# Input projection of twelve of sixteen token tiles in pieces inside the mixers; four tiles, key/value columns and compression in one first phase

## The reference

```python
h = rms_norm(x, norm_mix)
z = einsum('bsd,de->bse', h, w_in)                   # 2048 x 3096
(r_q, r_k, r_v, r_g, c_b, c_c, c_h, n_q, n_kc, n_vc, n_ks, n_vs, n_kw, n_vw, n_g) = split(z, ...)
y_ret = retention(r_q, r_k, r_v, r_g)                # 4 heads, chunks of 128, a state from chunk to chunk
y_conv = short_conv(c_b, c_c, c_h, conv_w)           # width 3
y_nsa = nsa(n_q, n_kc, n_vc, n_ks, n_vs, n_kw, n_vw, n_g, ...)
x = x + concat(y_ret, y_conv, y_nsa) @ w_out
x = x + relu(rms_norm(x, norm_mlp) @ w_up)**2 @ w_down
```

## Time and profile before

| | |
|---|---|
| time of runs | 3452.62 us (3452.37 to 3452.97) |
| profiled execution | 3461.74 us, its span 3459.8 us |
| projection | 0 to 583 us of the span |
| compression | 583 to 673 |
| mixers up to the first turned sum of a unit (L1436) | 673 to 797.1 |
| mixers, the next twenty units | 797.1 to 1401.8 |
| mixers, the rest | 1401.8 to 1777.6 |
| output product | 1777.6 to 2028 |
| MLP | 2028 to 3459.8 |
| mean granted TensorE clock | 0.949 of full |

### The profile page before, as it was taken

How to read it: one execution, slowest core, us unless ns; L and a number is a source line. 1 busy time by engine, 2 the same in 40 slices (tenths; PEclk the granted TensorE clock), 3 DMA queues, 4 the chain that set the end, 5 groups by cost and what they waited for, 6 DMA issues and landing times. The chain is left out here.

```text
span 3459.8 us, 43048 instructions
## 1 busy us (share of the span) xinstructions
PE 3198.2 (92%) x15500; PEld 2541.8 (73%) x15500; DVE 1480.1 (43%) x2760; ACT 984.4 (28%) x1621; POOL 1075.4 (31%) x614
## 2 busy tenths in 40 slices
PE   7999998668888899999979969999999999999999
PEld 7999998655555555565548758888788878888887
DVE  3113111046666666766532233336433543354333
ACT  3012000023434444444430032232222322232221
POOL 3222221043423323222010044444444434444442
PEclk9999999657989999999999979999999999999999
DMA  5223222210101001000023342223322232233221
GB/s 173 96 97 102 93 96 84 66 53 33 64 33 63 34 33 64 33 33 7 7 101 137 115 153 97 96 94 119 116 97 97 84 135 97 97 97 122 97 97 61
DMA packets 164983, 291.73 MB, mean 84 GB/s; under 512 B 19167, under 2 KB 126559, under 8 KB 162780
## 3 DMA queue, kind: packets, MB, share of 16 engines
q1 hardware_dynamic: 160252, 273.31, 23.2%
q10 hardware_dynamic: 4608, 16.78, 1.4%
HBM read 239.53 MB, written 50.53 MB: 84 GB/s over the span
## 5 line engine op out<-in xcount | busy, mean ns | idle before, releaser
L1756 POOL TENSOR_TENSOR mlp_down_lo<-mlp_down_raw,mlp_down_hi 128x2048 fp32r<-128x2048 f32 x64 | 298.3, 4661 | 750.5 <-ACT mlp_down_hi L1795 750.5
L1876 DVE TENSOR_TENSOR mlp_y<-mlp_acc,mlp_y 128x512 f32<-128x512 f32 x512 | 344.5, 688 | 201.3 <-PE mlp_acc L1954 196.4
L1954 PE MATMUL mlp_acc<-mlp_down_hi,mlp_f_hi 128*128 128x512 f32 x1024 | 402.4, 393 | 10.7 <-DVE mlp_y L1876 10.7
L1932 PE MATMUL mlp_up<-mlp_hT_hi,mlp_up_hi 128*128 128x512 f32 x1024 | 399.5, 390 | 2.5 <-DVE mlp_hT_lo L1898 2.5
L1954 PE MATMUL mlp_acc<-mlp_down_hi,mlp_f_lo 128*128 128x512 f32 x1024 | 400.0, 391 | 0.0
L1954 PE MATMUL mlp_acc<-mlp_down_lo,mlp_f_hi 128*128 128x512 f32 x1024 | 400.0, 391 | 0.0
L1932 PE MATMUL mlp_up<-mlp_hT_hi,mlp_up_lo 128*128 128x512 f32 x1024 | 399.3, 390 | 0.0
L1932 PE MATMUL mlp_up<-mlp_hT_lo,mlp_up_hi 128*128 128x512 f32 x1024 | 399.2, 390 | 0.0
L1863 DVE TENSOR_TENSOR mlp_f<-mlp_relu 128x512 f32<-128x512 f32 x128 | 133.2, 1042 | 603.2 <-ACT mlp_relu L1802 603.2
L311 PE MATMUL proj_acc<-proj_w_hi,proj_hT_hi 128*128 128x344 f32 x1152 | 369.8, 321 | 10.5 <-issue 9.5
L311 PE MATMUL proj_acc<-proj_w_hi,proj_hT_lo 128*128 128x344 f32 x1152 | 367.8, 319 | 0.0
(11 more groups left out here) (257 smaller groups left out, 5560.0 us busy)
## 6 DMA issues: line engine op xcount, KB each, us to landing
mlp_up_raw<-in_w_up SPq DMA_DIRECT2D x64, 1024.0 KB, 5.2
mlp_down_raw<-in_w_down SPq DMA_DIRECT2D x64, 1024.0 KB, 4.8
proj_w_raw<-in_w_in SPq DMA_DIRECT2D x18, 1376.0 KB, 6.4
z_scratch<-proj_z_out SPq DMA_DIRECT2D x144, 172.0 KB, 1.9
mix_z<-z_scratch SPq DMA_DIRECT2D x16, 1548.0 KB, 6.9
proj_x_tile<-in_x ACTq DMA_DIRECT2D x16, 512.0 KB, 3.9
mixed_scratch<-mix_mixed SPq DMA_DIRECT2D x16, 512.0 KB, 2.9
out_mixed<-mixed_scratch SPq DMA_DIRECT2D x16, 512.0 KB, 4.1
```

The lines of the kernel that those rows point to most:

```text
L1756: nc.gpsimd.tensor_tensor(dn_lo[:, b, :, :], dn_raw[:, :, :], dn_hi[:, b, :, :].bitcast(F32), ALU.subtract).then_inc(dn_lo_done, 1)
L1876: nc.vector.tensor_tensor(y[:, yb, tt, cols], acc[i % AR][:, :], y[:, yb, tt, cols], ALU.add).then_inc(added, 1)
L1932: mm = nc.tensor.matmul(up_ps[t % 2][:, :], w[:, b, k, cols], h[:, k, :], start=k == 0 and w is up_hi and h is h_hi, stop=k == KT - 1 and ...
L1954: mm = nc.tensor.matmul(acc[i % AR][:, :], a[:, b, k, tt * P:(tt + 1) * P], w[:, b, k, c * BANK:(c + 1) * BANK], start=k == 0 and a is f_h ...
```

## The change

**First phase.** `projection_phase` and `compress_phase` become one, `heads_phase`, again with a written list of steps, `HeadsPlan`. It normalises and transposes all sixteen tiles. Tiles 0 to 3 keep their transposed, split rows in SBUF and are multiplied with ten chunks of 284 columns: the 2840 columns of w_in other than n_kc, n_vc. For tiles 4 to 15 the transposed, split rows are stored to DRAM (`turned_scratch`, 1 MB a tile). Every chunk of w_in is loaded and split once, and both parts are stored (`split_scratch`, 2.3 MB a chunk). The 256 key/value columns are made for all tiles with the weights stationary, so that they come out transposed (`pair` steps: one group of four tiles, six of two); they are not stored. The compression steps stand among the last products; the bias rows ride as two more columns of `kvT`. The w1 of keys and of values share one buffer.

**Mixers.** The other 120 products (12 tiles x 10 chunks) are `fill` steps of the plan, each cut in four parts of 6 matmuls, with a `drain` (ACT) and a store (SP) behind it. They go two tiles at a time: two tiles of turned rows are held in SBUF (`held`), and each quarter of a chunk (`w_unit`, 0.58 MB, a ring of five) serves both tiles. 16 fills stand ahead of unit 0, and five in each unit after that until all are placed, which is in unit 20. They use `prep_ps`. z of a tile is loaded in parts (keys two deep, retention and convolution once), keys from tile 4 on only when all stores of its pair of tiles have landed. The prep pieces are sorted: key pieces of tile i + 2 in the unit with g = 0, retention pieces in the one with g = 1. Stores of `mixed` are cut in two. The constants are set and loaded at the start of this phase.

```diff
+T1 = 4
+CHUNKS = 10
+BW = 284
+class HeadsPlan:
+    def __init__(self, tiles):
+        groups = [range(0, 4)] + [range(t, t + 2) for t in range(T1, tiles, 2)]
+        products = [("product", c, t) for c in range(CHUNKS) for t in range(T1)]
+        later = iter(products)
+        for t in range(tiles):
+            steps.append(("tile", t))
+            for g, group in enumerate(groups):
+                if t == group[-1] + 1 or t == tiles - 1 == group[-1]:
+                    steps += [("pair", g, j) for j in range(2)]
+            if t >= T1 - 1:
+                steps.append(next(later))
+        rest = list(later)
+        spread = {1: ("bias rows",), 3: ("first", 0), 6: ("first", 1), 8: ("silu",), 9: ("second",),
+                  11: ("norm",), 13: ("turn",)}
...
 class Plan:
     def __init__(self, tiles):
-        self.steps = self.prep(0) + merge(first, self.prep(1))
+        self.steps = [("load keys", 0), ("load keys", 1), ("load retention", 0)] + self.more(2)
+        self.steps += self.spread(self.prep(0, KEY_PIECES), 2) + [("load keys", 2)]
+        early = self.prep(0, RET_PIECES) + [("store rows", 0), ("load retention", 1)] + self.prep(1, KEY_PIECES) + self.prep(1, RET_PIECES)
+        self.steps += merge(first, self.spread(early, FIRST_FILLS - 4))
...
-            ahead = []
-            if u + 2 < units:
-                pieces = self.prep(i + 2) if i + 2 < tiles else []
-                half = len(pieces) // GROUPS
-                ahead = merge(self.front(u + 2), pieces[g * half:(g + 1) * half])
+            pieces = self.prep(i + 2, (KEY_PIECES, RET_PIECES)[g]) if i + 2 < tiles else []
+            pieces = self.spread(pieces, UNIT_FILLS)
+            ahead = merge(self.front(u + 2), pieces) if u + 2 < units else pieces
+            if g == 0:
+                if i + 1 < tiles:
+                    self.steps.append(("store rows", i + 1))
+                if i + 2 < tiles:
+                    self.steps.append(("load retention", i + 2))
+                if i + 3 < tiles:
+                    self.steps.append(("load keys", i + 3))
...
+    def more(self, n):
+        while n > 0 and self.filled < self.fills:
+            steps += [("fill", self.filled, part) for part in range(PARTS)] + [("drain", self.filled)]
...
+    def spread(self, pieces, n):
+        gaps = [k for k, s in enumerate(pieces) if s[0] != "prep" or not s[2].startswith("read")] + [len(pieces)]
...
 PE of the mixers
+                if kind == "fill":
+                    n, part = step[1:]
+                    if part == 0:
+                        bank_free(("fill", n))
+                        pe.wait_ge(held_in[b], 16 * (pair + 1))
+                    pe.wait_ge(unit_in[unit % WS], 16 * (unit // WS + 1))
+                    for q in range(UNIT_K):
+                        nc.tensor.matmul(prep_ps[:, 0:BW], hi[:, k, :], w_hi[:, q, :], start=k == 0, stop=False)
+                        nc.tensor.matmul(prep_ps[:, 0:BW], lo[:, k, :], w_hi[:, q, :], start=False, stop=False)
+                        mm = nc.tensor.matmul(prep_ps[:, 0:BW], hi[:, k, :], w_lo[:, q, :], ...)
 ACT of the mixers
+                elif kind == "drain":
+                    act.wait_ge(fill_sum, n + 1)
+                    if n >= ZR:
+                        act.wait_ge(z_stored[n % ZR], 16 * (n // ZR))
+                    nc.scalar.copy(z_out[:, n % ZR, :], prep_ps[:, 0:BW]).then_inc(drained, 1)
```

More of the change, by code:

```diff
@@ L348, in chain, with clear_sems @@
+    def clear_sems(self, eng):
+        numbers = sorted(s.num for s in self.taken)
+        assert numbers == list(range(numbers[0], numbers[-1] + 1))
+        eng.sem_clear(range(numbers[0], numbers[-1] + 1))
 def chain(eng, done):
@@ new lines, in _ @@
+            nc.gpsimd.memset(values[:, :, :], 0.0).then_inc(values_cleared, 1)
+            pool.wait_ge(values_cleared, 1)
+            root(0)
+            pool.wait_ge(kv_hi_done, 1)
+            nc.gpsimd.tensor_tensor(kv_lo[:, :, :], w_raw[:, 1, :, 0:KV_WIDTH], kv_hi[:, :, :].bitcast(F32),
+                                    ALU.subtract).then_inc(kv_lo_done, 1)
+            root(1)
+            weights_low(0)
+            for step in plan.steps:
+                if step[0] == "tile":
+                    root(step[1] + 2)
+                elif step[0] == "product" and step[2] == 1:
+                    weights_low(step[1] + 1)
+                elif step[1:] == ("norm",):
+                    pool.wait_ge(cmp_squares, 1)
+                    link(nc.gpsimd.tensor_scalar(mean[:, :], ssq[:, :], 1.0 / HEAD, EPS, ALU.mult, ALU.add))
+                    nc.gpsimd.tensor_tensor(cmp_rstd[:, :], mean[:, :], neg_half[:, :], ALU.pow).then_inc(powered, 1)
@@ L642 @@
+    return m
 CMP, SLC, WIN = 0, 1, 2
@@ L705, in __init__ @@
                 self.steps.append(("post", u - 1, SLC))
+                if g == 0:
+                    self.steps.append(("store heads", i - 1))
             self.steps += own[1:5] + merge(own[5:] + [("values", u, SLC, i), ("lift", u, SLC)], ahead)
-        self.steps += [("turn", units - 1, SLC), ("post", units - 1, SLC)]
+        self.steps += [("turn", units - 1, SLC), ("post", units - 1, SLC), ("store heads", tiles - 1)]
+        assert self.filled == self.fills
+        self.bank_before = {}
+        before = None
+        for s in self.steps:
+            use = s if s[0] == "prep" and s[2].startswith("fill") else s[:2] if s[0] == "fill" else None
+            if use is not None and use != before:
+                self.bank_before[use] = before
+                before = use
         self.scores_n = {}
@@ L777, in mixers_phase @@
     NBLK = S // SLC_LEN
-    assert NBLK == NBLKS
+    KT = turned.shape[3]
+    assert NBLK == NBLKS and KT == PARTS * UNIT_K
     plan = Plan(NT)
@@ L1277, in _, with bank_free @@
         def _(pe):
-            pe.wait_ge(cleared, 1)
+            def bank_free(use):
+                before = plan.bank_before[use]
+                if before is not None:
+                    if before[0] == "fill":
+                        pe.wait_ge(drained, before[1] + 1)
+                    else:
+                        prep_read(pe, before[1], before[2][5:])
+            ready = False
             for step in plan.steps:
```

1288 lines of the change are left out of this document (727 added, 561 removed).

## The result

The changed kernel takes 3497.9 us (median of 4 runs, 3486.3 to 3504.2) beside 3452.8 for the kernel before (3452.4 to 3455.3). The ratio is 1.0125, 95% interval 1.0098 to 1.0153: slower by 45 us. The forecast was 3290, range 3205 to 3395. The profiled execution took 3499.9 us, its span is 3497.9. From here on, "unit" and "first finished unit" are cut at the same instructions as in the earlier trace rows: the first of the four transposes that turn a unit's selected branch.

What follows compares the result with a forecast made beforehand. TensorE was taken to wait for short VectorE and ScalarE chains early in the mixers and to be the bound late. 263 + 138 + 838 + 376 = 1615 for 1777.6, 163 less, gave 3290 us, range 3205 to 3395.

Steps and rivals of the forecast that it cites:

- Start of the first phase, tile part, products: 263: First phase, before the mixers: 23 start, 105 tiles 4 to 15, 125 products and compression, 10 last stores; was 673 us.
- Rival C: First phase bound by its transfers, 64.8 MB at 184 GB/s: 352 us, 89 more, total 3379; chance 0.10.
- To the first finished unit: 138: Mixers' start: 124.1 us becomes 138, as 23 + 37 + 57 + 21, with 21 fills added; ends 120 and 190.
- Units 1 to 20: 838: Mixers' units 1 to 20: 604.7 us becomes 838, as 481 work, 311 fills and 46 idle; ends 790 and 916.
- residual idle 2.3 a unit, 46: Units 1 to 20: TensorE idle left with fills in place, 2.3 us a unit, 46 us for 20 units.
- half of that comes back, 48: Units 1 to 20: 0.16 of the time at half clock; half of that is returned, 48 us.
- The work of 481: Units 1 to 20: work already there, 604.7 less 75.1 idle less 48 for the clock, 481 us.
- The lower count of 455: Units 1 to 20: work counted instruction by instruction at 227 and 112 ns, 455 us; used for the 790 end.
- rival D: Slower: fills' weight ring does not run ahead, 60 pairs each wait for a 5.2 us landing, 312 us; 3602; chance 0.05.
- 375.8 stays: Mixers from unit 21 to the end: unchanged at 375.8 us, since no fill is left and the bytes are the same.
- Rival A: Better cover: units at 790, start 125, first phase 250; 237 us less, 3216; chance 0.15.
- Rival B: Nothing is hidden: units 916, start 190, first phase 263; 33 us less, 3420; chance 0.08.

Runs made afterwards that it cites:

- The best version: Fastest run with all the work: the changed kernel with three edits of order, two of seven prep turns back in the first unit; 3364.4 us, ratio 0.9727.
- Turns shared: Against the kernel with three edits of order: two of the seven prep turns (qq and kz) moved back to the first unit's end; 3364.4 us, ratio 0.9727.
- three edits of order: Changed kernel with key/query turns in the second unit, projection chunk after next loaded earlier, and mixers' start loads reordered; 3370.9 us, ratio 0.9747.

## Why the prediction was wrong, step by step

- **Start of the first phase, tile part, products: 263, was 287.5.** I had named the load of a chunk behind the low part of the one before as a chain of 15.3 us beside 12.6 of matmuls, and charged 2.5 us a chunk for the last four. The queue's order cost 24 more at the fifth chunk, where the load stood behind loads that wait for memsets. With that line mended the phase ends at 263.2. The POOL and ScalarE times were right (4.96 and 2.1 us beside 5.1 and 2.1). Rival C, bound by transfers, is out: the DMA share is 0.68 over the phase and a line's move gave the time back.
- **To the first finished unit: 138, was 207.** Work (103 us at full speed) was right; 504 matmuls of fills at 131 ns and 280 others at 227 or 112 ns give 101. Idle was 76.5 where I had 35 (the 23 less three fills, and 21). Prep of tile 0 began 45 us behind the phase's start (332.6), where I had 23, and I had not seen that the drains wait for the tables too, so that fills can't run meanwhile. And I took full clock: it was 0.79, which by what is left of the 207 cost about 30. The best version still needs 179 to 186; the idle time left there is 54 to 56, and the clock 0.81 to 0.83. What of it could be had by other orders I did not try.
- **Units 1 to 20: 838, was 927.5. This is where the prediction failed**, in its term "residual idle 2.3 a unit, 46" and in "half of that comes back, 48". Idle was 99, and 46 us were lost to the half level, much as before the change (50). I argued that pieces of fills close the short waits and that a unit with 30 us of dense work keeps the clock. But the diff also sorts the prep pieces anew, and the sum has no term for that, not even one of nothing with its cover named. With the turns out of that unit the stretch is 855.7 at 51.8 idle and a clock of 0.98: the forecast's idle term and its returned clock, in a kernel with the order that I had silently assumed.
- **Prices.** The work of 481 held: TensorE was busy 828.5 us, and less 46 for the clock and 311 of fills that is 471. The lower count of 455 at the range's low end is wrong. At 227 ns for each matmul of 512 columns (890 of them) and 112 for the others it gives only about 390, and it leaves out that the 358 value matmuls cost more: here two of them and a score matmul (0.23) take 1.15 us, so one costs about 0.46.

```profile
1168.33 1.07 PE L1683 MATMUL mix_selected<-mix_probs,mix_v_s 128*66 128x512 f32 x2
1168.84 0.80 PE L1653 MATMUL mix_score<-mix_qa,mix_ka_s 97*128 97x512 f32 x1
1169.48 0.40 PE L1655 MATMUL mix_score<-mix_qb,mix_kb_s 128*128 128x512 f32 x1
```

The fill's 131 ns a matmul held (in a row they start 0.13 us apart, so 24 take 3.14 us). The quarter's landing, 5.3 us, was as in rival D's premise, and yet TensorE waited only 0.5 us for quarters in units 1 to 20. So D was wrong as a mechanism, though the sign it stood for came out:

```profile
mix_w_unit<-split_scratch SPq DMA_DIRECT2D x240, 568.0 KB, 5.3
```

- **Units 21 to the end: "375.8 stays" was wrong by 17.3.** The excess sits in the three units with the chain and the turns of keys and queries (41.0, 41.4 and 42.0 us where they took 33.7, 35.0 and 36.6), with the three waits for mix_q_pack. The old kernel with the same order has 377.9 for units 21 to 30. Turns shared brings it from 370.8 to 360.3; the kernel before has 353.1.
- **Rival A, better cover,** had 790 for the units; no version with whole fills came under 855. **Rival B, nothing hidden,** had 916 for the units and 190 for the start, near the measured 927.5 and 207, but for another reason: the fills hid 46 to 62 us, and the order lost as much again (58 in the old kernel, 72 here).

The condition for slower that I gave (TensorE waiting for quarters) was the wrong one. Over half of what was forecast can be had: with three edits of order and the turns shared or not, it is 88 to 94 us faster than before, where I had said 163. The rest of the difference is the start (41 to 48), units 1 to 20 (17 to 24) and the tail (7 to 12).

The granted clock went to 0.50, the lower of its two levels (1.2 GHz of 2.4), behind the 2.46 us wait shown above, and back to full at 1208 with TensorE busy again. The Trainium skill, TensorE: Matmul & The Clock Gate, section Part 1: The HAM clock gate, has it that the throttled state is the default and that activity releases it. By that rule, the trace agrees.

## What to carry to other kernels

When filler work is put into an in-order program, price what it does to the chains of the other engines: VectorE can't pass a step that waits for TensorE, so a long cross-engine chain and the step that ends it should stand a unit apart. When a change sorts steps anew in passing, test the sort in the old kernel by itself; here it cost 98 us, more than twice the change's whole loss. Filler hides short waits where it stands just before them, so spread it; in a row it hid nothing (327 us added to the 604.7 for 311 of matmuls) and cost 86 us.

## What the runs showed of the hardware

Short waits can cost as much again as they last, through the clock, even in dense stretches. A wait of 1.59 us at 1181 in the changed kernel was followed by 4 us at a clock of 0.58, one of 2.46 us at 1195.7 by some 10 us at 0.50 (rows above), in a unit in which TensorE was busy 48.3 of 55.3 us. I had expected such a unit to keep the full clock, as those of the earlier trace rows do. By the estimate above, the half level behind the nine waits for mix_q_pack costs 38 us, as much as the waits themselves (39.5). With spread fills and the turns a unit later, 30.7 us of units 1 to 20 are at the half level where it was 92.2.
